# Attention values of two heads multiplied in the two column halves of the array instead of one head at a time against zero-padded values

## What is computed

```python
out_r = (jnp.einsum("bkgnqm,bmkd->bnqkgd", p_meta, vm)
         + jnp.einsum("bkgnqj,bnjkd->bnqkgd", p_band, v_band)).reshape(B, S, H, Dh)
```

## Time and profile before

| | |
|---|---|
| time, median of 3 runs | 3276.88 us (3274.25 to 3279.68) |
| profiled execution | 3276.35 us |
| its span | 3274.8 us |
| PE busy | 3178.1 us (97%) |
| DVE busy | 2205.9 us (67%) |
| ACT busy | 1547.0 us (47%) |
| POOL busy | 333.4 us (10%) |
| chain that ended last | PE 85%, DVE 7%, ACT 2% |
| DMA | 342.42 MB, mean 105 GB/s |

### The profile page before, as it was taken

One profiled execution on the slowest core, in us unless ns is written; L12 is line 12 of the kernel. 1 busy time (PEld: TensorE's weight loads), 2 busy tenths in 40 slices (PEclk: granted clock), 3 DMA queues, 4 the chain that ended last, 5 costly groups with the idle time before them and its releaser, 6 DMA issues.

```text
span 3274.8 us, 59930 instructions
## 1 busy us (share of the span) xinstructions
PE 3178.1 (97%) x22102; PEld 2937.7 (90%) x22102; DVE 2205.9 (67%) x3031; ACT 1547.0 (47%) x2499; POOL 333.4 (10%) x341
## 2 busy tenths in 40 slices
PE   8999999999999999999979999999997999999997
PEld 7899999999999998888869999999997888887886
DVE  6677887888888886236785555556567555556647
ACT  5345555555555554232254544555236445555424
POOL 1000000000000001000001242240000214412000
PEclk9999999999999999999989999999998999999997
DMA  6244443344344345423243222223334222222422
GB/s 203 91 104 115 109 109 106 100 115 108 97 109 114 91 115 207 145 93 103 84 132 107 79 65 73 72 79 118 102 103 154 84 73 64 77 78 65 156 97 83
DMA packets 453738, 342.42 MB, mean 105 GB/s; under 512 B 20984, under 2 KB 445880, under 8 KB 450640
## 3 DMA queue, kind: packets, MB, share of 16 engines
q1 hardware_dynamic: 436032, 298.38, 30.9%
q0 software_dynamic: 8016, 24.83, 2.1%
q10 hardware_dynamic: 9552, 17.37, 1.5%
HBM read 315.04 MB, written 25.46 MB: 104 GB/s over the span
## 4 chain that ended last, share of the span: by engine, by line
PE 85%; DVE 7%; ACT 2%; DVEq 2%; issue 2%; DMA 1%; ACTq 0%; SPq 0%; POOL 0%
PE ps L681 16%; PE ps L682 16%; PE ps L683 15%; PE ps L851 8%; PE ps L854 8%; PE ps L853 8%; PE ps L1080 2%; PE ps L1121 1%; PE ps L921 1%; PE ps L687 1%; DVE w_low L1898 1%; PE ps L688 1%; PE ps L689 1%; DVE w_low_blocks L1988 1%; DVE residual L2364 1%
## 5 line engine op out<-in xcount | busy, mean ns | idle before, releaser
L681 PE MATMUL ps<-x_high,w_high 128*128 128x264 f32 (+3 forms) x3584 | 1179.8, 329 | 54.0 <-DVE w_low L1898 23.4
L682 PE MATMUL ps<-x_low,w_high 128*128 128x264 f32 (+3 forms) x3584 | 1149.8, 321 | 0.0
L683 PE MATMUL ps<-x_high,w_low 128*128 128x264 f32 (+3 forms) x3584 | 1146.7, 320 | 0.0
L681 PEld LDWEIGHTS ps<-x_high,w_high 128*128 128x128 f32 x3584 | 679.4, 190 | 113.8 <-issue 57.9
L1898 DVE TENSOR_TENSOR w_low<-w_raw,w_high 128x1024 fp32r<-128x1024 f32 x340 | 414.6, 1229 | 491.0 <-ACT w_high L1250 456.1
L682 PEld LDWEIGHTS ps<-x_low,w_high 128*128 128x128 f32 x3584 | 679.6, 190 | 53.2 <-issue 3.3
L683 PEld LDWEIGHTS ps<-x_high,w_low 128*128 128x128 f32 x3584 | 678.4, 189 | 49.2
L1250 ACT ACTIVATE w_high<-w_raw 128x1024 fp32r<-128x1024 f32 x340 | 358.7, 1057 | 323.7 <-PE ps L683 295.7
L851 PE MATMUL ps<-x_high,w_high_blocks 128*128 128x256 f32 x1600 | 456.3, 285 | 0.0
L854 PE MATMUL ps<-x_high,w_low_blocks 128*128 128x256 f32 x1600 | 449.3, 281 | 0.0
L853 PE MATMUL ps<-x_low,w_high_blocks 128*128 128x256 f32 x1600 | 449.2, 281 | 0.0
(11 more groups left out here) (443 smaller groups left out, 4191.5 us busy)
## 6 DMA issues: line engine op xcount, KB each, us to landing
w_raw_blocks<-in_w_in SPq DMA_DIRECT2D x200, 512.0 KB, 4.9
w_raw<-in_w_in SPq DMA_DIRECT2D x384, 256.0 KB, 3.1
w_raw<-in_w_out SPq DMA_DIRECT2D x280, 256.0 KB, 3.0
residual<-residual_stream ACTq DMA_DIRECT2D x8, 1056.0 KB, 11.4
residual_stream<-y_layer ACTq DMA_DIRECT2D x2, 2176.0 KB, 10.2
x_natural<-in_x SPq DMA_DIRECT2D x4, 1024.0 KB, 9.2
x_feature_major<-x_stage POOLq DMA_DIRECT2D x4, 1024.0 KB, 6.6
y_sgu_feature_major<-z_silu_g POOLq DMA_DIRECT2D x8, 512.0 KB, 5.0
```

The costliest lines, as they stand in the source:

```text
L681: pe.matmul(dst, wh[:, j, kt, wc], xh[:, k, tok], start=first, stop=False)
L682: pe.matmul(dst, wh[:, j, kt, wc], xl[:, k, tok], start=False, stop=False)
L683: return pe.matmul(dst, wl[:, j, kt, wc], xh[:, k, tok], start=False, stop=last)
```

## The change

The values of the two heads of a pair are multiplied in one place, `value_pair(c)`, at step 14 for heads 0 and 1 and at step 22 for heads 2 and 3. For each key block there are two products with 64 value columns, one per head, alternating: head `h` reads its own transposed probabilities and writes partitions `h * HD` to `(h + 1) * HD` of bank 7. The values are kept without zero columns (`v_group`), so the MEMSET of the zeros goes. `pv_done` rises by two at the end of a pair.

```diff
-        vz = rr.take("v_zero_padded", [P, ST, 3 * HD])
+        vz = rr.take("v_group", [P, ST, HD])
...
-                    def value(i):
-                        c = i // 2
-                        if i % 2 == 0:
-
-                            pe.wait_ge(o_taken, 2 * G + c)
-                        if i == 0:
+                    def value_pair(c):
+
+                        pe.wait_ge(o_taken, 2 * G + c)
+                        if c == 0:
                             pe.wait_ge(vz_ready, G + 1)
-                        pe.wait_ge(pt_evac, 4 * A + 4 * i + 4)
-                        v0 = 0 if i % 2 else HD
+                        pe.wait_ge(pt_evac, 4 * A + 8 * c + 8)
                         for b in range(ST):
                             e = min(b + 2, ST)
-                            last = pe.matmul(ps[:, 7, b * BLK:e * BLK], vz[:, b, v0:v0 + P],
-                                             pts[i % 2][:, 2 * b * BLK:(b + e) * BLK], start=(i % 2 == 0 and b == 0),
-                                             stop=False, skip_group_check=True)
-                        if i == 3 and not real:
+                            for h in range(2):
+                                pe.matmul(ps[h * HD:(h + 1) * HD, 7, b * BLK:e * BLK], vz[:, b, :],
+                                          pts[h][:, 2 * b * BLK:(b + e) * BLK], start=(b == 0),
+                                          stop=False, skip_group_check=True)
+                        if c == 1 and not real:
                             meta_queries(1)
-                        if i % 2:
-                            y = y2[:, ds(Y_ATT + 2 * g + c, 1), 0:S].squeeze(1)
-                            last = pe.matmul(ps[:, 7, :], vm[:], y, start=False, stop=True, skip_group_check=True)
-                        last.then_inc(pv_done, 1)
+                        y = y2[:, ds(Y_ATT + 2 * g + c, 1), 0:S].squeeze(1)
+                        pe.matmul(ps[:, 7, :], vm[:], y, start=False, stop=True, skip_group_check=True).then_inc(pv_done, 2)
...
-                        if k >= 10 and k % 4 == 2:
-                            value((k - 10) // 4)
+                        if k in (14, 22):
+                            value_pair((k - 14) // 8)
...
-                            act.activation(vz[:, 2 * q:2 * q + 2, HD:2 * HD], v2[:, 1:3, ds(H0 * q + HD * g, HD)], ACT.Copy)
+                            act.activation(vz[:, 2 * q:2 * q + 2, :], v2[:, 1:3, ds(H0 * q + HD * g, HD)], ACT.Copy)
...
-                dve.memset(vz[:], 0.0)
```

## The result

| | before | changed | ratio (95% interval) |
|---|---|---|---|
| median | 3276.88 us | 3257.36 us (3254.92 to 3259.29, 5 runs) | 0.9941 (0.9926 to 0.9957) |
| profiled execution, span | 3274.8 us | 3253.4 us | |

Of five runs of the kernel before, one took 3923.89 us; it is left out of the ratio, and the median of the other four is 3275.70. The change gains 19.5 us by the medians in the table, 0.6%, and 18.3 by that one; both kernels run again side by side had 3277.06 and 3257.71 us, a gain of 19.4. Forecast were 3256 us and a gain of 20.6.

The account below looks back on a forecast made before the run. PE, busy 97% of the span, was taken to bound the kernel. Sixteen pairs saving 1.29 us each give 20.6 us, switches and the rest nothing: 3276.35 - 20.6 = 3255.8, said as 3256 us; range 3250 to 3278.

Parts of the forecast that it names:

- What bounds the kernel: In the head groups of both layers PE is busy nearly throughout, so the end moves with its instructions one for one.
- The slack at steps 10 and 18: PE reaches the transposes of heads 1 and 3 1.51 us sooner; the smaller slack, 5.1 us, becomes 3.6: covered.
- The price of before: Value products at line 1121: 1.51 us a head, seven slots of 0.216 us, 48.3 us for 32 heads.
- The overlap: Value pairs: both array halves stream at once, started in program order; 1.73 us a pair instead of 3.02, saving 20.6 us.
- The other bound given for 1.73: Feeding each MATMUL with its load takes 0.11 us, as in the transposes; 16 of them take 1.76 us a pair.
- Switching at 0: Two changes between full-width and 64-column products a pair, 32 in all, were claimed to cost nothing.
- the gate rows: Gate products at the start, three 64-column MATMULs then four full-width transposes: period 1.13 us, parts 1.14, so switches looked free.
- The upper bound named beside it: A change of form costs at most a value MATMUL's tail, 0.163 us; 32 of those would be 5.2 us.
- A: Rival at the value pairs: halves overlap, but each change of form drains, 5.2 us in all; 3261 us, chance 0.12.
- B: Rival at the value pairs: pieces of different halves collide on what they read, half the gain; 3266 us, chance 0.08.
- C: Rival at the value pairs: halves take turns, 3.02 us a pair; 3276 us, or 3281 with A's drains, chance 0.17.
- D: Rival at the value pairs: weight loads not hidden beside streams, 0.14 us for each MATMUL, 35 us slower; 3311 us, chance 0.08.

## Why the prediction was right, step by step

**What bounds the kernel**: right. PE had almost nothing to wait for in the groups, and PE time taken out came out of the total (18.6 us in the pairs by the rows, 19.5 measured). The slack at steps 10 and 18 and at the groups' ends held; no wait grew by more than 0.4 us.

**The price of before**: right. 1.51 us a head, and 3.04 us for two that follow each other.

**The overlap**: right in kind, mis-sized in the term. The prediction put MATMULs in program order within a slot, which leaves an offset of one slot, 8 slots and 1.73 us a pair. PE started the odd piece past the waiting even one: 7 slots, 1.51 us. The other bound given for 1.73, that load and MATMUL cannot be fed faster than the transposes' 0.11 us, is refuted only by the last block: there a couple, two MATMULs with their loads, follows the last after 0.11 us (1817.28 to 1817.39), 0.055 each. The couples of 256 columns, 0.216 us for two, are just what that bound allows. That both bounds gave 1.73 was no confirmation of either.

**Switching at 0**: wrong. It rested on the gate rows, and those are fp32r; the values are fp32. The upper bound named beside it, the tail of 0.163 us a change, was nearly the price: 0.35 us a pair for two changes, 0.15 to 0.18 each in the runs with 64 of them. The rule of the Trainium skill cited there (TensorEngine Tiling (Array Packing), Key Properties: a change of tiling mode drains the engine) agrees with the fp32 products of this trace and not with the fp32r ones. The prediction let one row outvote it without asking whether the row was of the same kind.

The two errors cancel in part: 0.22 us a pair too much and 0.35 too little leave 1.16 us gained where 1.29 was forecast, 2 us in all. So the time was met to 1.4 us (3256 against 3257.36) by a sum with two wrong terms, which is luck. The range and the signs do not rest on that; the number's last two microseconds do.

**The rivals**: A's drains are real, but at 5.6 us they stand against a larger gain than A assumed (24.2 - 5.6 = 18.6, not 15.4). B (part of the overlap) and C (turns) are refuted by starts 0.01 us apart and a full couple every 0.216 us; C is what the run with both heads on the same half shows (3281.54; forecast for C with drains 3281). D is refuted by the loads: between the edges, two loads of 0.14 us lie beside each couple (those of 1817.28 and 1817.29, beside the couple that starts at 1817.28). The rule of the Trainium skill that the prediction named there (TensorE: Matmul & The Clock Gate, Part 3, The mechanism: a weight load overlaps running MATMULs only where the row groups differ) does not hold for the halves of this kernel, which use all rows.

## What to carry to other kernels

In this kernel two fp32 products with 64 output columns each, written to different partition halves, cost the time of one; the same products on one half, or on 128 padded columns, cost two. Budget 0.15 to 0.18 us for each change between full-width and fp32 half-width work, so gather such products: the 32 heads alone at their own steps lost 11.5 us here, while the 16 pairs gained 19.5. Alternate the halves, with no more than two fp32 products (four MATMULs) of one half in a row: three cost 7.7 us here, four about 16. And before a row is used as the price of something else, compare its data type as well as its shape.

## What the runs showed of the hardware that was not expected

- PE starts MATMULs of one column half ahead of up to three waiting MATMULs of the other half that precede them in the program (5th with the 1st, 7th with the 3rd, 9th with the 5th). The Trainium skill, TensorE: Matmul & The Clock Gate, Part 3, The mechanism, states that MATMULs start and end strictly in program order; these rows show otherwise, and the measurement decides.
- A change of form costs 0.15 to 0.18 us with fp32 on 64 columns and nothing measurable with fp32r on 64 columns (period 1.13 us for parts of 1.14). Why the data type decides stays open; fp32r products on the upper half were not tried.
- Two fp32 streams of 256 columns at once do not slow each other: 0.216 us a slot, as one alone.
